# First stage of a hybrid trunk with a second activation buffer inside the weight region

## The reference

```
ada = silu(c) @ w_ada + b_ada                      # 6 x 1024 modulation values
h   = rms_norm(x, norm1_gain) * (1 + sc1) + sh1    # scaled and shifted input
p   = h @ w_in                                     # 5*1024 plain + 3*1024 + 64 + 64 + 128 shifted columns
...                                                # gated conv branch, RWKV-7 branch (chunked recurrence), merge
x   = x + g1 * (merged @ w_out)
x   = x + g2 * moe(rms_norm(x, ...) * (1 + sc2) + sh2)   # 32 experts, top 2
out = rms_norm(x, final_gain)
```

## Time and profile before

| | |
|---|---|
| median of 3 runs (lowest, highest) | 4411.86 us (4409.42, 4412.15) |
| the profiled execution | 4404.34 us, span 4402.5 us |
| busy shares over the span | PE 91%, DVE 42%, ACT 30%, POOL 11% |
| DMA traffic over the span | 760.52 MB, mean 173 GB/s |
| first matmul of the second stage | 196.12 us |

### The profile page before, as it was taken

One profiled execution on the slowest core, in us unless ns is written; L12 is line 12 of the kernel. 1 busy time (PEld: TensorE's weight loads), 2 busy tenths in 40 slices (PEclk: granted clock), 3 DMA queues, 4 the chain that ended last, 5 costly groups with the idle time before them and its releaser, 6 DMA issues.

```text
span 4402.5 us, 93154 instructions
## 1 busy us (share of the span) xinstructions
PE 4022.2 (91%) x36187; PEld 2801.7 (64%) x36187; DVE 1843.2 (42%) x3765; ACT 1332.3 (30%) x2995; POOL 468.1 (11%) x519
## 2 busy tenths in 40 slices
PE   5699999999999999999999999999779999999992
PEld 3477787787787787777777778755444444444440
DVE  3345555555555555555545545532521111111115
ACT  3223333343343343343333333343301111111114
POOL 1001201201201201200200200100000000000003
PEclk8799999999999999999999999999889999999996
DMA  9621221212212212212212212223289999999999
GB/s 328 222 67 50 84 66 57 84 52 71 84 42 81 84 42 81 84 42 81 83 44 78 84 45 70 87 83 133 77 349 411 411 411 411 411 411 411 411 411 374
DMA packets 292930, 760.52 MB, mean 173 GB/s; under 512 B 16466, under 2 KB 107828, under 8 KB 292532
## 3 DMA queue, kind: packets, MB, share of 16 engines
q1 hardware_dynamic: 273876, 687.60, 42.1%
q0 software_dynamic: 11520, 41.95, 2.4%
q10 hardware_dynamic: 7136, 25.23, 1.4%
HBM read 679.19 MB, written 75.52 MB: 171 GB/s over the span
## 4 chain that ended last, share of the span: by engine, by line
PE 85%; issue 5%; DVE 3%; SPq 2%; DMA 2%; ACT 2%; DVEq 0%; POOL 0%; ACTq 0%; POOLq 0%
PE duo L1057 24%; PE bank L1057 10%; PE bank L1417 10%; PE bank L1421 5%; PE bank L1447 5%; PE bank L1287 5%; PE bank L1451 3%; PE duo L1186 2%; PE duo L1184 2%; PE duo L1163 2%; PE duo L1157 1%; PE bank L1120 1%; PE bank L1104 1%; PE duo L1398 1%; PE bank L1106 1%
## 5 line engine op out<-in xcount | busy, mean ns | idle before, releaser
L1057 PE MATMUL duo<-hs,w 128*128 128x256 f32 x5120 | 1141.3, 381 | 28.1 <-ACT at L1483 25.4
L1057 PEld LDWEIGHTS duo<-hs,w 128*128 128x128 f32 x5120 | 969.1, 190 | 220.1 <-issue 33.8
L1057 PE MATMUL bank<-hs,w 128*128 128x256 f32 x2048 | 462.9, 379 | 0.0
L1417 PE MATMUL bank<-W,xT 128*128 128x512 f32 x1024 | 446.4, 594 | 2.2 <-DVE xT L2476 1.5
L1057 PEld LDWEIGHTS bank<-hs,w 128*128 128x128 f32 x2048 | 389.1, 190 | 52.9
L1417 PEld LDWEIGHTS bank<-W,xT 128*128 128x128 f32 x1024 | 192.7, 191 | 233.3 <-issue 233.3
L1483 ACT ACT_TABLE_LOAD x254 | 325.9, 1283 | 11.1 <-issue 6.1
L2482 DVE TENSOR_TENSOR gsig<-bank,gsig 128x512 f32<-128x512 f32 x48 | 33.2, 692 | 675.2 <-ACT gsig L1483 675.2
L819 POOL TENSOR_TENSOR Tm<-Tm,idents 128x512 f32<-128x512 f32 x32 | 40.5, 1267 | 1966.7 <-DVE Tm L2191 1966.7
L1421 PE MATMUL bank<-W,xT 128*64 128x512 f32 x1024 | 228.6, 602 | 18.8 <-issue 18.8
L1287 PE MATMUL bank<-wo,mT 128*128 128x512 f32 x512 | 231.8, 599 | 0.0
(11 more groups left out here) (409 smaller groups left out, 6297.6 us busy)
## 6 DMA issues: line engine op xcount, KB each, us to landing
W<-in_w_expert_in_dram SPq DMA_DIRECT2D x128, 2048.0 KB, 25.4
W<-in_w_expert_out_dram SPq DMA_DIRECT2D x64, 2048.0 KB, 25.4
hs<-h_s SPq DMA_DIRECT2D x224, 512.0 KB, 4.5
w<-in_w_in_dram SPq DMA_DIRECT2D x128, 256.0 KB, 4.2
adaw<-in_w_ada_dram SPq DMA_DIRECT2D x12, 2048.0 KB, 13.3
y_s<-ysb ACTq DMA_DIRECT2D x48, 512.0 KB, 6.7
xt<-in_x_dram SPq DMA_DIRECT2D x16, 512.0 KB, 11.6
WAc<-rank_s SPq DMA_DIRECT2D x32, 256.0 KB, 3.2
```

The lines of the kernel that those rows point to most:

```text
L1057: ins = mm(place(pr, n), w[:, pr, n, k, :], hs[:, n, k, :], start=n < 4 and k == 0, stop=k == KH - 1, skip_group_check=True)
L1417: ins = mm(GU[half][:, :], xT[:, slot, kk_, :], ring_rows(parts[0])[:, k, cols], start=kk_ == 0, stop=kk_ == KT - 1)
```

## The change

The groups get two activation buffers: even groups keep `hg`, odd groups use the first 4096 values of each partition in `w[:, 2:4]`, where the weights of pairs 2 and 3 lie later. `evac_x` of group g then waits for group g - 2, and no longer for group g - 1. The sums of groups 2 and 3 go into `xt[:, 0]` and `xt[:, 1]`; those of groups 0 and 1 into `hs[:, 0:4]`, so that `mix_h(1)` gets a wait of its own for the save of group 0. The loads of pairs 2 and 3 move behind the whole stage, and the reload of `hs` waits for two saved groups where it waited for three.

```diff
@@ -485,11 +485,17 @@
         def h_mixed(g):
-            return hs[:, 0:4] if g < NG - 1 else xt[:, 1].rearrange("p j (k t) -> p j k t", k=KH)
-        def h_quarter(kh, th):
-            return hg[:, kh * KH:kh * KH + KH, th * GH:th * GH + GH]
+            return hs[:, 0:4] if g < 2 else xt[:, g % 2].rearrange("p j (k t) -> p j k t", k=KH)
+        def h_group(g):
+            if g % 2 == 0:
+                return hg
+            return w[:, 2:4].rearrange("p a b c d -> p (a b c d)")[:, 0:KT * G].rearrange("p (k t) -> p k t", t=G)
+        def h_quarter(g, kh, th):
+            return h_group(g)[:, kh * KH:kh * KH + KH, th * GH:th * GH + GH]
         PLACE = ((0, 1), (0, 0), (1, 0), (2, 0), (0, 0), (1, 0), (2, 0))
@@ -544,7 +550,7 @@
                 sp.wait_ge(S["T_act"], 4 * g + 4)
                 sp.wait_ge(S["T_dve"], 4 * g + 4)
                 for slot, kh, th in ((U_B11, 0, 0), (U_B21, 1, 0), (U_B22, 1, 1)):
-                    sp.dma_start(h_s[g, slot].rearrange("p (k t) -> p k t", k=KH), h_quarter(kh, th))\
+                    sp.dma_start(h_s[g, slot].rearrange("p (k t) -> p k t", k=KH), h_quarter(g, kh, th))\
                         .then_inc(S["h_saved"], 16)
                 sp.wait_ge(S["h_mix"], 4 * g + 4)
                 for j, slot in enumerate((U_T2, U_T1, U_T3, U_T4)):
@@ -582,11 +588,11 @@
             sp.wait_ge(S["rank_saved"], 32)
             sp.dma_start(WAc[:, :], rank_s[0, :, 0:G]).then_inc(S["wa_in"], 16)
             sp.dma_start(GDc[:, :], rank_s[1, :, 0:G]).then_inc(S["gd_in"], 16)
-            for pr in range(4):
+            for pr in range(2):
                 load_pair(pr, 0)
             for g in range(1, NG):
                 if g == NG - 1:
-                    sp.wait_ge(S["h_saved"], 16 * NPROD * g)
+                    sp.wait_ge(S["h_saved"], 16 * NPROD * 2)
                     for n in range(NPROD):
                         load_h(0, n)
                 save_h(g)
@@ -598,6 +604,9 @@
             sp.dma_start(ada_s, ada48[:, :]).then_inc(S["ada_trip"], 16)
             sp.wait_ge(S["rank_saved"], 32 * NG)
             sp.wait_ge(S["h_saved"], 16 * NPROD * NG)
+            sp.wait_ge(S["rank_done"], 2 * NG)
+            for pr in range(2, 4):
+                load_pair(pr, 0)
             def load_step(ct, g, final=False):
                 i = ct * NG + g
@@ -949,7 +958,7 @@
                     if g:
                         pe.wait_ge(S["rank_mixed"], 2 * (g - 1) + m + 1)
                     for k in range(KT):
-                        ins = mm((M0, M1)[m][:, :], wrank[:, k, m * P:m * P + P], hg[:, k, :],
+                        ins = mm((M0, M1)[m][:, :], wrank[:, k, m * P:m * P + P], h_group(g)[:, k, :],
                                  start=k == 0, stop=k == KT - 1)
                     ins.then_inc(S["rank_done"], 1)
@@ -1509,13 +1518,13 @@
                 fn(xst[:, 2, cols], xst[:, 1, cols], ACT.Exp, scale=-0.5).then_inc(S["rstd"], 4)
             def evac_x(g):
-                if g:
-                    act.wait_ge(S["rank_done"], 2 * g)
-                    act.wait_ge(S["h_mix"], 4 * g)
-                    act.wait_ge(S["h_saved"], 16 * NPROD * g)
+                if g >= 2:
+                    act.wait_ge(S["rank_done"], 2 * g - 2)
+                    act.wait_ge(S["h_mix"], 4 * g - 4)
+                    act.wait_ge(S["h_saved"], 16 * NPROD * (g - 1))
                 for k in range(0, KT, 2):
                     act.wait_ge(S["tr_done"], KT * g + k + 1)
-                    fn(hg[:, k, :], TB[k % 4][:, :], ACT.Identity,
+                    fn(h_group(g)[:, k, :], TB[k % 4][:, :], ACT.Identity,
                        scale=modc[:, 0, k:k + 1], bias=modc[:, 1, k:k + 1]).then_inc(S["T_act"], 1)
             def rank_scale(g, m):
@@ -1920,20 +1929,22 @@
                         .then_inc(S["xn_ready"], 1)
             def evac_x(g):
-                if g:
-                    dve.wait_ge(S["rank_done"], 2 * g)
-                    dve.wait_ge(S["h_saved"], 16 * NPROD * g)
+                if g >= 2:
+                    dve.wait_ge(S["rank_done"], 2 * g - 2)
+                    dve.wait_ge(S["h_saved"], 16 * NPROD * (g - 1))
                 for k in range(1, KT, 2):
                     dve.wait_ge(S["tr_done"], KT * g + k + 1)
-                    V.tensor_scalar(hg[:, k, :], TB[k % 4][:, :], modc[:, 0, k:k + 1],
+                    V.tensor_scalar(h_group(g)[:, k, :], TB[k % 4][:, :], modc[:, 0, k:k + 1],
                                     modc[:, 1, k:k + 1], ALU.mult, ALU.add).then_inc(S["T_dve"], 1)
             def mix_h(g):
                 dve.wait_ge(S["T_act"], 4 * g + 4)
                 dve.wait_ge(S["T_dve"], 4 * g + 4)
-                if g == NG - 1:
-                    dve.wait_ge(S["tr_done"], KT * NG)
-                b11, b12, b21, b22 = (h_quarter(kh, th) for kh in range(2) for th in range(2))
+                if g == 1:
+                    dve.wait_ge(S["h_saved"], 16 * NPROD)
+                if g >= 2:
+                    dve.wait_ge(S["tr_done"], KT * (g + 1))
+                b11, b12, b21, b22 = (h_quarter(g, kh, th) for kh in range(2) for th in range(2))
                 t2, t1, t3, t4 = (h_mixed(g)[:, j] for j in range(4))
                 V.tensor_tensor(t1, b12, b11, ALU.subtract).then_inc(S["h_mix"], 1)
                 V.tensor_tensor(t3, b22, b12, ALU.subtract).then_inc(S["h_mix"], 1)
```

## The result

The changed kernel takes 4379.93 us (median of 4 runs, 4377.15 to 4381.54) against 4410.64 us for four runs of before: ratio 0.9926, 95% interval 0.9913 to 0.9939. It is faster by 0.74%, 30.7 us (26.9 to 38.4 by the interval); the forecast was 4377 us. Six further runs on another occasion (first experiment) gave 34.8 us. The profiled execution has a span of 4376.8 us.

What follows compares the result with a forecast made beforehand. The first stage was taken as bound by a save, evacuation and `rout` loop that idles DMA. Buffer 28 us plus weights 7.2 us gave 35 off 4411.9: 4377 us, range 4374 to 4381, with run spread and profile offset 4367 to 4384.

Steps and rivals of the forecast that it cites:

- What bounds the stage: First 230 us: saves, evacuations, `rout` and SP form one loop; the prize is idle DMA time, 31.0 us.
- the three waits: ACT's waits for saves of `hs` before evacuating the next group's first bank, 45.7 us in all.
- The second buffer, 28 us of 31: Waiting for group g - 2 instead of g - 1 recovers 28 us of idle DMA time, at most 31.
- the place called tightest: Group 1's `rout`, ready by 64.2 us, 2.4 us before group 0's last save lands and DMA runs dry.
- the signs of being right: Group 1 evacuates at about 58 us, no DMA window under 280 GB/s, no SP `rout` waits, second stage near 161 us.
- The new wait of `mix_h(1)`, nothing: DVE's added wait for group 0's save at 66.6 us costs nothing; uncovered, a few us.
- The 14 us of slack at each group: Compute slack in the first stage, said to exceed the few us on DVE if the `mix_h(1)` wait were uncovered.
- The weights, 7.2 us: Eight loads, 2.10 MB at 290 GB/s, leave the DMA-bound first stage: 7.2 us gained.
- the sum's 35: 28 us from the buffer plus 7.2 from the weights: 35 us off, bounds 28 and 38.2.
- The cover of the late loads: Second stage's start: pairs 2 and 3 ready after 14 and 19 us, third pair starts at 29.2 us; cost nothing.
- POOL beside DVE, under 0.5 us: Late pairs' POOL sums meeting DVE's first second-stage work cost under 0.5 us, covered; by the lock, 10 us at most.
- The rivals: Stop stays, 4387 or 4397 us (0.12); slower transfers, 4385 (0.10); no real change, 4405 (0.05); slower, 4428 at 80 us (0.03).

Runs made afterwards that it cites:

- first experiment: The changed kernel run once more with no edit: 4367.81 us (6 runs) against 4402.56 us for 17 runs of before, ratio 0.9921.
- old-traffic kernel: The changed kernel plus eight 256 KB loads into unread places, where pairs 2 and 3 loaded before: median 4378.08 us, ratio to before 0.9942.

## Why the prediction was right, point by point

*What bounds the stage.* Right: the prize was the time in which the DMA engines idled around the three waits, not the waits' 45.7 us. The old-traffic kernel shows it from the other side, since useless bytes put back cost their price and a little more (8.2 to 8.9 us for 7.2).

*The second buffer, 28 us of 31.* Right: 28.3 us. The DMA engines did not run dry at the place called tightest: `rout` came at 62.2 us, 2 us ahead of the 64.2 of the estimate. SP's waits for `rout` did not all go, as the signs of being right had it: one of 4.1 us is left, just there (41.9 us in three before), with the engines at 405 GB/s meanwhile. One wait was missing from this step. `rout` is a single buffer too, and ACT waited 9.86 us for group 1's `rank_s` save before it could write group 2's `rout`:

```profile
104.83 1.27 ACT L1492 ACTIVATE rout<-rmx 64x512 f32<-64x512 f32 x2 [9.86 <-DMA rank_s<-rout]
```

Evacuations started at 56.7, 78.7 and, behind this wait, 106.9 us, not at 58, 81 and 104. The wait cost nothing, because SP came for group 2's `rout` only at 118.2 us, 4.9 us after it was made.

*The new wait of `mix_h(1)`, nothing.* Right for the stage: DVE waited 2.95 us there for group 0's save, and SP came for these sums only at 91.2 us. The 14 us of slack at each group, by which the step prices the loss of its cover, are not worked out from rows; the margins that the prediction does work out, 93 against 87 and 116 against 110 us, are 6.

*The weights, 7.2 us.* Right, with 7.2 taken away from the kernel before and 8.2 to 8.9 put back into the changed one. Together with the buffer 36.5 to 37.3 us, above the sum's 35 and near the upper bound of 38.2.

*The cover of the late loads.* Right: 27.9 us of cover for 12.1 us of work, and 11.5 us of PE standing once the cover is cut.

*POOL beside DVE, under 0.5 us.* Right for the sums that it priced, wrong in what it looked at, though nothing came of it. I looked at pairs 2 and 3 in the second stage, where the sums did stay at 1.3 us, and at POOL's rows alone. The pairs that collided were 0 and 1: with the stage shorter, their sums fell on DVE's sums of group 2 and scalings of group 3, and DVE lost 1 us in each of two sums and 4 in four scalings. The Trainium skill, "SBUF — State Buffer", section "SBUF: two separate sides", has the lock that the prediction cites, and this trace agrees (2.29 us beside POOL, 1.22 apart). It cost no time because compute had slack to the transfers.

*The rivals.* None happened. No stop stayed: from 62.5 to 152.5 us the slowest of the 5-us windows ran at 310 GB/s, in the weight loads. Transfers held 379 GB/s over 62.5 to 155 us, weight rows included. That speaks against a ceiling at the 358 GB/s which the Trainium skill, "DMA: Bandwidth & Descriptors", section "Bandwidth", gives for transfers with memory; the same section ties that figure to both cores of a pair streaming, and this kernel runs on one.

*The total.* The stage gave 36.5 us and the first four runs 30.7, whose interval (26.9 to 38.4 us) holds both. That the rest moves forward unchanged was right for the work but not for each execution's time: the second stage's length varies by several us, and in both pairs of profiles it was longer where more time fell at half clock. With 17 runs of before spreading over 4394.87 to 4413.59 us, my spread of 3 us was too small. That the median came within 3 us of 4377 is in part luck: on the other occasion the two kernels took 4402.56 and 4367.81 us, and the second lies at the lower edge of the stated 4367 to 4384. Why a given step gets such a stretch in one execution and not in the next stays open; no run here changed it on purpose.

## What to carry to other kernels

A wait of 45 us on a transfer is worth the time in which the transfer engines idle during it, which a table of GB/s by window gives; here that and the bytes moved out of the stretch forecast its end to about 2 us. In a stage bound by bytes, a second buffer pays once and each byte moved under later compute pays again, as long as the cover is counted up to the last helper (here POOL's sums). When a stage gets shorter, check which engines' work now coincides, on both sides of a possible collision, and which other single buffer (here `rout`) now holds the loop.

## What the runs showed of the hardware that I had not expected

The same program's second stage and tail took between 4206.4 and 4219.4 us in two executions of before. TensorE's granted clock drops to its lower level (half, 1.2 of 2.4 GHz) for short stretches in different steps each time: 0.96 over a step of 83.87 us and 1.00 over the same step of 80.46 us. A gain of 8 us in one stage is therefore readable in the profile's timeline, within a us, long before the total shows it.

DVE and POOL working on SBUF at the same time slowed both: POOL's weight sums went from 1.27 us to as much as 2.25 and DVE's from 1.22 to 2.29, while DVE's scalings, with one tensor input, went from 0.75 to 1.75. Not every meeting did this: beside POOL's sums of pairs 2 and 3 (163.94 to 174.30 us), DVE ran instructions such as `su<-su,duo`, with an input in PSUM, with pauses between them, and POOL's sums took 1.26 to 1.31 us. No run here separates the pauses from the kind of instruction.
